# Three projections advanced together, tile by tile, at the three places where a hybrid decoder kernel starts from a freshly split activation

## The reference, cut to what matters

```python
xn = rms_norm(h, norm_pre_mix)
proj = xn @ w_in                       # hgrn, attention and gla heads
...                                    # recurrences and dilated window attention
h = h + rms_norm(mix, norm_post_mix)
u = jnp.square(jax.nn.relu(rms_norm(h, norm_pre_mlp) @ w_up))
h = h + rms_norm(u @ w_down, norm_post_mlp)
h = h + jax.nn.sigmoid(h @ w_ple_gate) * (p_i @ w_ple)
```

## Time and profile before

| | us |
|---|---|
| median of 3 runs | 2100.69 |
| lowest and highest run | 2096.72 and 2100.75 |
| the profiled execution's own time | 2097.26 |
| its span, first to last instruction | 2095.7 |

### The profile page before, as it was taken

One profiled execution on the slowest core, in us unless ns is written; L12 is line 12 of the kernel. 1 busy time (PEld: TensorE's weight loads), 2 busy tenths in 40 slices (PEclk: granted clock), 3 DMA queues, 4 the chain that ended last, 5 costly groups with the idle time before them and its releaser, 6 DMA issues. The chain is left out here.

```text
span 2095.7 us, 35698 instructions
## 1 busy us (share of the span) xinstructions
PE 1924.8 (92%) x15744; PEld 1721.2 (82%) x15744; DVE 850.7 (41%) x1267; ACT 636.2 (30%) x937; POOL 72.9 (3%) x88
## 2 busy tenths in 40 slices
PE   5999998888799999997979999988797999999977
PEld 4977876558699999997968768765596999999967
DVE  5322445433632433335444133455427323333353
ACT  4321112444432322232344111125534222222232
POOL 0002002000000000000000020020000000000000
PEclk9985897999899999998989859969998999999989
DMA  7321404862282736251152231068514638255312
GB/s 275 111 91 42 133 1 155 294 241 81 74 300 88 275 127 209 101 183 61 54 182 80 84 122 50 2 217 311 182 60 154 238 103 303 86 201 171 120 46 95
DMA packets 71521, 298.74 MB, mean 143 GB/s; under 512 B 5696, under 2 KB 27968, under 8 KB 69696
## 3 DMA queue, kind: packets, MB, share of 16 engines
q1 hardware_dynamic: 63936, 196.11, 26.7%
q0 software_dynamic: 7424, 100.27, 13.7%
HBM read 288.11 MB, written 108.53 MB: 189 GB/s over the span
## 5 line engine op out<-in xcount | busy, mean ns | idle before, releaser
L1410 PE MATMUL pair<-x_hi_part,w_hi_part 128*128 128x288 f32 x1536 | 464.3, 302 | 47.2 <-DVE x_lo_part L1585 47.1
L1411 PE MATMUL pair<-x_lo_part,w_hi_part 128*128 128x288 f32 x1536 | 458.6, 299 | 0.0
L1412 PE MATMUL pair<-x_hi_part,w_lo_part 128*128 128x288 f32 x1536 | 456.8, 297 | 0.0
L1410 PEld LDWEIGHTS pair<-x_hi_part,w_hi_part 128*128 128x128 f32 x1536 | 292.7, 191 | 57.8 <-issue 41.2
L1410 PE MATMUL pair<-u_hi_part,w_hi_part 128*128 128x288 f32 x1024 | 303.1, 296 | 0.0
L1411 PE MATMUL pair<-u_lo_part,w_hi_part 128*128 128x288 f32 x1024 | 302.1, 295 | 0.0
L1412 PE MATMUL pair<-u_hi_part,w_lo_part 128*128 128x288 f32 x1024 | 301.1, 294 | 0.0
L1412 PEld LDWEIGHTS pair<-x_hi_part,w_lo_part 128*128 128x128 f32 x1536 | 294.5, 192 | 0.0
L1411 PEld LDWEIGHTS pair<-x_lo_part,w_hi_part 128*128 128x128 f32 x1536 | 293.9, 191 | 0.0
L1585 DVE TENSOR_TENSOR w_lo_part<-raw,w_hi_part 128x1024 fp32r<-128x1024 f32 x160 | 196.0, 1225 | 166.8 <-ACT w_hi_part L1478 166.8
L1478 ACT ACTIVATE w_hi_part<-raw 128x1024 fp32r<-128x1024 f32 x160 | 168.8, 1055 | 241.6 <-PE pair L1412 241.6
(11 more groups left out here) (209 smaller groups left out, 2613.6 us busy)
## 6 DMA issues: line engine op xcount, KB each, us to landing
raw<-w_units SPq DMA_DIRECT2D x202, 512.0 KB, 3.5
ck_out<-ck POOLq DMA_DIRECT2D x16, 3060.0 KB, 14.4
cv_out<-cv POOLq DMA_DIRECT2D x16, 3060.0 KB, 23.1
arena<-ck SPq DMA_DIRECT2D x8, 1920.0 KB, 8.0
more<-ck SPq DMA_DIRECT2D x8, 1920.0 KB, 11.1
arena<-cv SPq DMA_DIRECT2D x8, 1920.0 KB, 13.3
tail<-cv SPq DMA_DIRECT2D x8, 1920.0 KB, 10.1
raw<-w_first SPq DMA_DIRECT2D x12, 512.0 KB, 4.9
```

What stands on the lines that cost most here:

```text
L1410: nc.tensor.matmul(out, wh[:, cols], xh[:, k, t], start=n == 0, stop=False)
L1411: nc.tensor.matmul(out, wh[:, cols], xl[:, k, t], start=False, stop=False)
L1412: mm = nc.tensor.matmul(out, wl[:, cols], xh[:, k, t], start=False, stop=n == KT - 1)
```

## The change

At each of the three starts the first three units (`hf0`, `hf1`, `gq1`; `up0` to `up2`; `gate0` to `gate2`) advance together. In step `s`, PE does tile `s` of the first unit, tile `s - 1` of the second and tile `s - 3` of the third (`BEHIND`), after one wait for activation tile `s`. The third unit accumulates in pair 2 (`APART`, `home`), which is free then. For the first projections, weight units 1 and 2 are split on ACT and DVE before the normalisation and not after it. And `z0`, `z1` come after `hq0` and not before it, in PE's order, in ACT's order and in `LIN`.

```diff
+TOGETHER = 3
+BEHIND = (0, 1, 3)
+APART = ("gq1", "up2", "gate2")
...
+        def home(name):
+            return pair[2 if name in APART else Q[name] % 2]
...
+                    for name in IN1[0:2]:
+                        claim(name)
+                    pe.wait_ge(w_split, TOGETHER)
+                    for s in range(KT + BEHIND[-1]):
+                        if s < KT:
+                            pe.wait_ge(x_split, s + 1)
+                        for u, lag in enumerate(BEHIND):
+                            if 0 <= s - lag < KT:
+                                mm = steps(home(IN1[u]), w_part(wh_sb, u), w_part(wl_sb, u), s - lag)
+                                if s - lag == KT - 1:
+                                    mm.then_inc(lin_mm, 1)
...
                         mm.then_inc(lin_mm, 1)
-                        if name == "gq1":
+                        if name == "hq0":
                             pe.wait_ge(s_par0, 16)
                             pe.wait_ge(lin_ev, Q["gq1"] + 1)
...
                     nc.scalar.preload_act_table_set("natural_log_exp_and_others")
-                    split_w(0)
+                    for i in range(TOGETHER):
+                        split_w(i)
...
-                    split_w(1)
-                    split_w(2)
...
+                    evac("hq0", proj["hq0"])
+                    split_w(6)
                     act.wait_ge(s_par0, 16)
                     evac("z0", LV[1][:, 0], ACT.Identity, bias=par[:, W_B:W_B + 1])
                     evac("z1", LV[1][:, 1], ACT.Identity, bias=par[:, W_B + 1:W_B + 2])
-                    evac("hq0", proj["hq0"])
-                    split_w(6)
...
                     total("sum_mlp", 2)
+                    claim("up0")
+                    claim("up1")
+                    pe.wait_ge(side_ev, KT)
+                    together([(f"up{j}", I_UP + j) for j in range(TOGETHER)], 2 * KT)
...
+                    claim("gate0")
+                    claim("gate1")
+                    pe.wait_ge(side_ev, len(SIDE))
+                    together([(f"gate{k}", I_GATE + k) for k in range(TOGETHER)], 3 * KT)
+                    for k in range(TOGETHER, KT):
+                        split_product(claim(f"gate{k}"), I_GATE + k, XH, XL, lin_mm)
```

More of the change, by code:

```diff
@@ L69 @@
 SMALL = [l for l, h in enumerate(LEVELS) if 2 * h <= DEC_SEQ]
-LIN = (["sum_pre", "hf0", "hf1", "gq1", "z0", "z1", "hq0", "hq1", "gq0", "gk0", "gk1"]
+LIN = (["sum_pre", "hf0", "hf1", "gq1", "hq0", "z0", "z1", "hq1", "gq0", "gk0", "gk1"]
        + ["vs0", "vs1"]
@@ L408, in _, with steps @@
                     mm.then_inc(lin_mm, 1)
+                    def steps(ps, wh, wl, k):
+                        cols = slice(k * P, (k + 1) * P)
+                        for half in range(2):
+                            out, t = ps[:, half, 0:HALF], slice(half * HALF, (half + 1) * HALF)
+                            nc.tensor.matmul(out, wh[:, cols], XH[:, k, t], start=k == 0, stop=False)
+                            nc.tensor.matmul(out, wh[:, cols], XL[:, k, t], start=False, stop=False)
+                            mm = nc.tensor.matmul(out, wl[:, cols], XH[:, k, t], start=False, stop=k == KT - 1)
+                        return mm
+                    for name in IN1[0:2]:
[9 more added lines that the diff above has]
+                                    mm.then_inc(lin_mm, 1)
                     for i, name in enumerate(IN1):
+                        if i < TOGETHER:
+                            continue
                         ps = claim(name)
@@ L413, in _ @@
                         for k in range(KT):
[L414 to L421, removed]
+                            mm = steps(ps, wh, wl, k)
                         mm.then_inc(lin_mm, 1)
-                        if name == "gq1":
+                        if name == "hq0":
                             pe.wait_ge(s_par0, 16)
@@ L462, in evac @@
                         act.wait_ge(lin_mm, Q[name] + 1)
-                        A(two(dst), pair[Q[name] % 2][:, :, 0:HALF], func, **kw).then_inc(lin_ev, 1)
+                        A(two(dst), home(name)[:, :, 0:HALF], func, **kw).then_inc(lin_ev, 1)
                     def leading(dst, src, done):
@@ L1424, in claim_side, with together @@
                         return pair[2 + q % 2]
+                    def together(units, ready):
+                        pe.wait_ge(w_split, units[-1][1] + 1)
+                        for s in range(KT + BEHIND[-1]):
+                            if s < KT:
+                                pe.wait_ge(x_split, ready + s + 1)
+                            for (name, i), lag in zip(units, BEHIND):
+                                k = s - lag
+                                if not 0 <= k < KT:
+                                    continue
+                                wh, wl, cols = w_part(wh_sb, i), w_part(wl_sb, i), slice(k * P, (k + 1) * P)
+                                for half in range(2):
+                                    out, t = home(name)[:, half, 0:HALF], slice(half * HALF, (half + 1) * HALF)
+                                    nc.tensor.matmul(out, wh[:, cols], XH[:, k, t], start=k == 0, stop=False)
+                                    nc.tensor.matmul(out, wh[:, cols], XL[:, k, t], start=False, stop=False)
+                                    mm = nc.tensor.matmul(out, wl[:, cols], XH[:, k, t], start=False, stop=k == KT - 1)
+                                if k == KT - 1:
+                                    mm.then_inc(lin_mm, 1)
                     def total(name, ready):
@@ L1456, in _ @@
                     total("sum_mlp", 2)
+                    claim("up0")
+                    claim("up1")
+                    pe.wait_ge(side_ev, KT)
+                    together([(f"up{j}", I_UP + j) for j in range(TOGETHER)], 2 * KT)
                     for c in range(CHUNKS):
                         i = I_UP + 2 * KT * c
-                        for j in range(KT):
-                            first_ = c == 0 and j == 0
-                            split_product(claim(f"up{c * KT + j}"), i + j, XH, XL, lin_mm, (x_split, 2 * KT) if first_ else None)
+                        for j in range(TOGETHER if c == 0 else 0, KT):
+                            split_product(claim(f"up{c * KT + j}"), i + j, XH, XL, lin_mm)
                         for n in range(KT):
@@ L1465, in _ @@
                     total("sum_down", 3)
-                    for k in range(KT):
-                        split_product(claim(f"gate{k}"), I_GATE + k, XH, XL, lin_mm, (x_split, 3 * KT) if k == 0 else None)
+                    claim("gate0")
[4 more added lines that the diff above has]
+                        split_product(claim(f"gate{k}"), I_GATE + k, XH, XL, lin_mm)
                 @block.scalar
@@ L1539, in _ @@
                             act.wait_ge(lin_mm, Q[f"up{g}"] + 1)
-                            A(two(TMP[g % 2]), pair[Q[f"up{g}"] % 2][:, :, 0:HALF], ACT.Relu).then_inc(lin_ev, 1)
+                            A(two(TMP[g % 2]), home(f"up{g}")[:, :, 0:HALF], ACT.Relu).then_inc(lin_ev, 1)
                             split_w(i + SPLITS)
@@ L1571, in _ @@
                         act.wait_ge(lin_mm, Q[name] + 1)
-                        A(two(TMP[k % 2]), pair[Q[name] % 2][:, :, 0:HALF], ACT.Sigmoid).then_inc(lin_ev, 1)
+                        A(two(TMP[k % 2]), home(name)[:, :, 0:HALF], ACT.Sigmoid).then_inc(lin_ev, 1)
                         split_w(I_GATE + k + SPLITS)
```

2 lines of the change are left out of this document (removed).

## The result

| | before | changed |
|---|---|---|
| median of the runs shown first, us | 2098.7 (4 runs, 2093.98 to 2100.75) | 2071.82 (4 runs, 2069.07 to 2075.55) |
| profiled execution: own time, us | 2097.26 | 2072.45 |
| span, us | 2095.7 | 2070.9 |

The ratio is 0.9883, with a 95% interval from 0.9859 to 0.9907.

What follows compares the result with a forecast made beforehand. PE, busy 92% of the span, loses time to activation-tile waits and half-pace matmuls. Terms 5.1 + 5.85 + 5.9 + 2.0 + 0.9 = 19.75 us take the median 2100.69 to 2080.9; predicted 2080, range 2073 to 2090.

Steps and rivals of the forecast that it cites:

- Up: First three up units: PE waits for no tile after the first, 21.0 us against 23.55; 2.55 us less per layer.
- Gate: First three gate units: 21.3 us, with later tile waits and the clock's fall gone; 5.85 and 5.9 us less.
- First projections: Group of hf0, hf1, gq1 at 21.0 us, starting 2.0 and 1.0 us later for early splits; 0.5 and 1.5 us left.
- z0 and z1: Stop around the small products, now behind hq0: 2.7 us instead of 3.16, minus 0.45 us in each layer.
- The clock behind z: Fall of PE's clock after z1, left as it is; if it went, each layer would give 1.5 us more.
- What is queued behind: Unit 3's weights after each group: 4.8 us of PE work covers about 3.1 us of preparation, so no new wait.
- Three open pairs at no cost: Changes of unit in the six stages cost nothing; from the other side they could cost 13 us.
- The forecast fall of the waits: PE's waits for `x_lo_part`, activation tiles from DVE, fall from 47.1 us by some 12 us or more.
- the clock taking it back: Rival: PE's clock stays at its lower level throughout the six groups, 81 us slower, 2162 us; chance 0.04.
- new waits: No-change rival: unit 3's weights are late by as much as the group ends earlier; 2097 to 2101 us, chance 0.03.
- More than the sum: Rival: clock's fall after z1 goes in both layers (3 us) and it rises sooner in some stages; 2071 to 2076, chance 0.11.

Runs made afterwards that it cites:

- up_only: The kernel before with only up0 to up2 together, first projections and gate as before; ratio 0.9964 (0.9952 to 0.9977).
- gate_only: The kernel before with only gate0 to gate2 together, first projections and up as before; ratio 0.9956 (0.9939 to 0.9973).
- early_splits: The kernel before with only weight units 1 and 2 of the first projections split ahead of the normalisation; one execution, 2100.47 us.
- among: The change with the splits of weight units 1 and 2 among the first projections' activation tiles and PE's tile order written out; ratio 0.9871, median 2066.86.
- z_old: The change with z0 and z1 ahead of hq0, as in the kernel before; ratio 0.9915 (0.9895 to 0.9936).
- no_lag: The change with the three units level, lags 0, 0, 0 instead of 0, 1, 3; ratio 0.9958, median 2089.41.
- two: The change with two units together (lags 0 and 1), the third after them, in all three places, early weight splits kept; ratio 0.9892 (0.9875 to 0.9908).
- first_only: The kernel before with only the first projections as in the change, z0 and z1 behind hq0, up and gate as before; ratio 0.9984 (0.9973 to 0.9995).

## Why the prediction was right, point by point

The change was forecast as faster by 19.75 us with the time at 2080, and measured by the medians 26.9 us faster in the first set and 22.5 in the second, at 2071.8 and 2072.6. The sign, the mechanism and most terms hold. Both medians lie just under the range of 2073 to 2090, by 1.2 and 0.4 us. A part of that is the starting point: the forecast set out from 2100.69, and the kernel before measured 2098.7 and 2095.08 in these sets. The ratio of 0.9883, applied to 2100.69, gives 2076.1, inside the range and 4 us under the forecast. The gain itself was forecast 3 to 7 us too small; the terms below say where.

- **Up**, forecast 2.55 in each layer: 2.7. PE waits for no tile after the first. The term was slightly small because the half-pace beginning has 14 to 15 matmuls here and I took 16. Shown by `up_only`.
- **Gate**, forecast 5.85 and 5.9: 5.75 and 5.77. The 0.4 us wait for tile 1, the rise of the clock about 4 us after the start and the missing second fall are all in the timeline. Shown by `gate_only`. What the fall had cost was priced at 1.5 us; the gate of `up_only` that had none, and a late rise instead, was 1.1 us shorter.
- **First projections**, forecast 0.5 and 1.5: the stretch to the v products, less the 0.67 us of the next point and the 1.5 us of the clock behind z in the second layer, gives 0.8 and 1.2. The group took 22.0 us there instead of 21.0, as its clock rose only 6.1 us after the start. The first matmul moved by 2.0 us in the first layer, as worked out. In the second it moved by 0.3 and 1.1 us in two profiles of the change and 0.7 with the splits alone, for a forecast of 1.0. `early_splits` shows the shift, `among` that it could be avoided.
- **z0 and z1**, forecast 0.45 each for the stop: 0.67 in the profile, and the 2.7 us was 2.61. The forecast's 3.16 us for the stop before was read from 0.12 us after the last matmul's start; from start to start it is 3.28. But that is the difference of the whole change to the kernel before. Within the change the step is worth 2.3 to 2.8 us in each layer (`z_old`), which I had not seen.
- **The clock behind z**, left as it was: it falls in the changed kernel's first layer and not in its second, 1.5 us. In the kernel before it was also absent in one layer of the repetition. It changes from execution to execution.
- **What is queued behind**, 4.8 us of cover against 3.1: no wait for unit 3 in the change, and `no_lag`, which cuts the cover to 1.6, brings a wait of 1.6 us at each place. Shown.
- **Three open pairs at no cost**: groups run at 0.133 us a matmul with every sixth going to another pair, so the changing of pairs alone costs nothing. The Trainium skill (TensorE: Matmul & The Clock Gate, "A second HAM failure mode: psum-queue depth-cycling") puts the swing of the clock down to brief idling of PE between groups of matmuls in a kernel that goes through the banks in turn; the groups here have no idle time after their first matmul but the wait for tile 1 in gate. Only `two` had some of it, two more waits of 0.2 us in gate, and its clock held; longer idling with pairs in turn was not run. In the 36 groups with the change's lags or the written-out order that were profiled, the clock never fell between its rise and the group's end.
- **The forecast fall of the waits** for `x_lo_part` by 12 us or more was too large: it is 9.5 us. It could not have been 12: the first waits, which stay, are 37.2 of the 47.1 us (two of 8.6, two of 4.0 and two of 5.95), which leaves 9.9. A good part of the groups' gain is matmuls at full clock and not waiting.

What the sum lacked: `sum_down` at full pace, 1.0 us in each layer, which comes with the shorter up stage (shown by the profiles, not its cause), the clock behind z in one layer, 1.5 us, and the clock in the mixer. The mixers give 1.5 us in the profiled pair and 3.7 us between the two repetitions, but the kernel before alone moves by 1.1 us in its two profiles, and the change by 3.3. How much of the 22.5 to 26.9 us belongs to the mixer is open; the terms that the profiles show, without it, are 23.6, and 1.5 of these are the clock behind z.

The rivals: no case of the clock taking it back, and none of new waits. "More than the sum" is nearest to what happened: its 2071 to 2076 us holds both medians. I had named the clock behind z in both layers and an earlier rise for it; the first came in one layer, and `sum_down` I had not seen. That the time fell there is in part luck, since the clock behind z and the mixers move by some us between executions.

## What to carry to other kernels

Where a product starts from tiles that come slower than one output tile can use them, start several output tiles together; two were enough here, and the third gave 0.9 us at the slowest source. Let them end apart by at least the time that the next unit's preparation takes, and look at what the other engines have queued where the ends move together: an evacuation that used to be prompt may stand behind work for the neighbouring unit. If preparations have to be moved ahead for it, put them among the first tiles and give PE other work meanwhile; here that gave about 3 us in the profiled stretches, which the runs alone do not separate.

## What the runs showed of the hardware that was not expected

The four matmuls of `sum_down` follow the same 4.1 us wait in both kernels and yet run at half pace in one (2.26 us) and faster in the other (1.26 us), in 13 layers each way. The moment at which the clock rises after a group's first matmul went from 3.0 us (25.78 to 28.77, the first projections of `first_only`, first layer) to 6.1 us (1047.18 to 1053.28, the changed kernel's, second layer), with no wait in either group. With gate's units one after another it took 4.3 us in seven of ten profiled layers, 8 us in one and 14 us in two (`up_only`, `first_only`). A mixer of identical instructions took from 331 to 340 us, with granted clocks from 0.83 down to 0.80. Differences of 2 to 3 us between two versions of this kernel can therefore not be read from a single time.
